# Gathering the token rows of a mixture of experts with three bf16 products in place of one fp32 product

## The reference

```python
lg = t @ wg                                  # 4 group logits
gi = argmax(lg); gp = softmax(lg)[gi]        # one group for each token
le = (t @ we).reshape(S, 4, 8)[gi]           # 8 expert logits of that group
tv, ti = top_k(softmax(le), 2)               # two experts for each token
cw = one_hot(gi * 8 + ti) * (tv / sum(tv) * gp)
gu = einsum('sd,edf->sef', t, w_gu)
hid = silu(gu[..., :256]) * gu[..., 256:] * cw
y = einsum('sef,efd->sd', hid, w_down)
```

## Time and profile before

| what | us |
|---|---|
| median of 3 runs | 1324.32 |
| lowest and highest | 1315.74, 1326.11 |
| profiled execution, time | 1324.0 |
| profiled execution, span on the core | 1321.8 |
| PE busy | 1131.9 (86%) |
| DVE busy | 542.0 (41%) |
| ACT busy | 341.3 (26%) |
| POOL busy | 56.4 (4%) |
| mean granted clock of PE | 0.938 of 2.4 GHz |

### The profile page before, as it was taken

How to read it: one execution, slowest core, us unless ns; L and a number is a source line. 1 busy time by engine, 2 the same in 40 slices (tenths; PEclk the granted TensorE clock), 3 DMA queues, 4 the chain that set the end, 5 groups by cost and what they waited for, 6 DMA issues and landing times.

```text
span 1321.8 us, 23637 instructions
## 1 busy us (share of the span) xinstructions
PE 1131.9 (86%) x9653; PEld 659.4 (50%) x9653; DVE 542.0 (41%) x1424; ACT 341.3 (26%) x650; POOL 56.4 (4%) x66
## 2 busy tenths in 40 slices
PE   5579998878887968689999999789795899999995
PEld 2146665556666935444444444567572534444433
DVE  3431194424341162624444444524337235444434
ACT  1112240121111211323233332234303233323322
POOL 2000000000000000000001000000000000000100
PEclk9789998999898979789999999899797999999997
DMA  8533115776775054009999996300622089999941
GB/s 249 171 127 121 71 64 177 277 258 238 259 261 205 4 221 191 1 10 425 421 425 425 423 417 249 135 12 1 255 103 89 0 349 423 428 426 420 422 199 40
DMA packets 45977, 297.21 MB, mean 225 GB/s; under 512 B 5956, under 2 KB 7336, under 8 KB 22344
## 3 DMA queue, kind: packets, MB, share of 16 engines
q1 hardware_dynamic: 43856, 290.17, 55.3%
q0 software_dynamic: 1840, 5.79, 1.9%
q10 hardware_dynamic: 200, 0.06, 0.0%
HBM read 293.77 MB, written 2.24 MB: 224 GB/s over the span
## 4 chain that ended last, share of the span: by engine, by line
PE 75%; DMA 11%; DVE 9%; ACT 2%; issue 2%; SPq 0%; ACTq 0%; DVEq 0%; POOL 0%; POOLq 0%
PE bank L686 73%; DMA ring<-in_ada_w 9%; DVE work L1501 2%; DMA ring<-in_kv_ada_w 2%; ACT work L1245 1%; DVE work L1507 1%; DVE work L1504 1%; DVE rstd L1539 1%; DVE x_res L1874 1%; DMA ring<-in_rw_w_rkv 1%; PE bank L1064 1%; DVE work L1860 1%; DVE ring L1501 1%; DVE work L1613 0%; PE bank L1231 0%
## 5 line engine op out<-in xcount | busy, mean ns | idle before, releaser
L686 PE MATMUL bank<-ring,work 128*64 128x512 f32 (+1 forms) x1760 | 351.3, 552 | 9.3 <-DVE work L1860 7.6
L686 PE MATMUL bank<-work,ring 128*128 128x320 f32 (+3 forms) x1600 | 302.0, 367 | 30.6 <-DVE work L1501 8.4
L686 PEld LDWEIGHTS bank<-work,ring 128*128 128x128 f32 (+2 forms) x1600 | 214.0, 173 | 118.5 <-issue 30.6
L686 PE MATMUL bank<-work 128*128 128x320 bf16 (+7 forms) x1906 | 227.0, 284 | 41.8 <-DVE work L1781 13.9
L686 PEld LDWEIGHTS bank<-ring,work 128*64 128x64 f32 (+1 forms) x1760 | 118.9, 138 | 218.3 <-issue 211.2
L686 PEld LDWEIGHTS bank<-work 128*128 128x128 bf16 (+3 forms) x1906 | 166.8, 126 | 113.2 <-issue 39.7
L1245 ACT ACTIVATE work<-bank 128x320 f32<-128x320 f32 (+6 forms) x111 | 55.8, 537 | 252.4 <-PE bank L686 235.8
L686 PE MATMUL bank<-ring 64*64 64x64 f32 (+2 forms) x2624 | 103.8, 233 | 2.1 <-issue 2.1
L686 PEld LDWEIGHTS bank<-ring 64*64 64x64 f32 (+2 forms) x2624 | 94.1, 144 | 21.8 <-issue 18.0
L686 PE MATMUL bank<-ring,cs 128*32 128x512 f32 x448 | 64.5, 661 | 39.9 <-DMA ring<-in_ada_w 33.9
L1874 DVE SCALAR_TENSOR_TENSOR x_res<-bank,mod,x_res 128x256 f32<-128x256 f32 (+1 forms) x256 | 86.1, 378 | 16.8 <-PE bank L686 2.7
(11 more groups left out here) (185 smaller groups left out, 754.3 us busy)
## 6 DMA issues: line engine op xcount, KB each, us to landing
ring<-in_moe_w_gu SPq DMA_DIRECT2D x64, 2048.0 KB, 13.5
ring<-in_moe_w_down SPq DMA_DIRECT2D x64, 1024.0 KB, 14.0
ring<-in_ada_w SPq DMA_DIRECT2D x40, 1024.0 KB, 5.3
ring<-in_rw_w_rkv SPq DMA_DIRECT2D x6, 2048.0 KB, 8.0
ring<-in_ada_w SPq DMA_DIRECT2D x4, 2048.0 KB, 28.6
ring<-in_kv_ada_w SPq DMA_DIRECT2D x8, 1024.0 KB, 4.9
ring<-in_rw_w_o SPq DMA_DIRECT2D x2, 2048.0 KB, 11.5
ring<-in_at_w_q SPq DMA_DIRECT2D x2, 2048.0 KB, 14.1
```

Source lines behind the costliest of these rows:

```text
L686: return eng.matmul(out, l, r, start=start, stop=stop, **kw)
```

## The change

`htok` is no longer an operand of a product. It is split into three bf16 parts, `hpart`, that add up to it: part 2 is `htok` rounded to bf16 (ACT), the remainder is written over `htok` (GpSimd), part 1 is the remainder rounded to bf16 (ACT), and part 0 is what is left after that (GpSimd). `pick` becomes bf16. PE multiplies each part by `pick` and adds up nine products in a bank where it added three, and it goes through the parts as its outer loop, so it opens all eight banks of a half before the first product. ACT makes part 2 of a token tile right behind the two copies of that tile, and takes the two exponentials behind tile 1 in place of behind tile 2.

```diff
@@ views
+        hpart = work[:, 0:9 * D // 2].bitcast(BF16).rearrange("p (s j d) -> p s j d", s=3, j=3)
-        pick = work[:, off[0]:off[0] + 3 * ROWS].rearrange("p (j s) -> p j s", j=3)
+        pick = work[:, off[0]:off[0] + 3 * ROWS // 2].bitcast(BF16).rearrange("p (j s) -> p j s", j=3)
@@ GpSimd, cleared(l)
                 pl.did(eng.memset(htok[64:128, 2, :], 0.0), ("htok padded", l))
+                pl.settle()
+                for j in range(3):
+                    pl.wait("hpart", l, 2, j)
+                    pl.did(eng.tensor_tensor(htok[:, j, :], htok[:, j, :], hpart[:, 2, j, :], ALU.subtract),
+                           ("hrest", l, j))
+                for j in range(3):
+                    pl.wait("hpart", l, 1, j)
+                    pl.did(eng.tensor_tensor(hpart[:, 0, j, :], htok[:, j, :], hpart[:, 1, j, :], ALU.subtract),
+                           ("hpart", l, 0, j))
@@ TensorE, moe(l)
                 for hf in range(2):
-                    for c in range(C):
-                        pb = bank.open("rows", l, c, hf)
-                        for j, (t0, kt) in enumerate(TILES):
-                            if c == 0:
-                                if hf == 0:
-                                    pe.wait("htok ready", l, j, 1)
-                                    if j == 2:
-                                        pe.wait("htok padded", l)
-                                pe.wait("picked", l, hf, j)
-                            ins = mm(pb[:, 0:T], htok[:, j, P * c:P * c + P], pick[:, j, T * hf:T * hf + T],
-                                     j == 0, j == 2)
-                        full(ins, "rows", l, c, hf)
+                    pbs = [bank.open("rows", l, c, hf) for c in range(C)]
+                    for part in (2, 1, 0):
+                        for c in range(C):
+                            for j in range(3):
+                                if c == 0:
+                                    pe.wait("hpart", l, part, j)
+                                    pe.wait("picked", l, hf, j)
+                                ins = mm(pbs[c][:, 0:T], hpart[:, part, j, P * c:P * c + P],
+                                         pick[:, j, T * hf:T * hf + T], part == 2 and j == 0, part == 0 and j == 2)
+                            if part == 0:
+                                full(ins, "rows", l, c, hf)
@@ ScalarE, moe(l)
                     for hf in range(2):
                         act(hrow[0:k, j, 64 * hf:64 * hf + 64, :],
                             pk("htok", l, j, hf)[0:k, :].rearrange("p (q c) -> p q c", c=C), ACT.Copy,
-                            ("read", "htok", l, j, hf), ("htok ready", l, j, hf))
-                ac.wait("group max", l)
-                ac.wait("top2", l)
-                act(rt[:, 6:9, 0:4], rt[:, 3:6, 0:4], ACT.Exp)
-                act(rt[:, 36, 0:3], rt[:, 35, 0:3], ACT.Exp, ("route exp", l))
+                            ("read", "htok", l, j, hf))
+                    if j == 2:
+                        ac.wait("htok padded", l)
+                    ac.settle()
+                    act(hpart[:, 2, j, :], htok[:, j, :], ACT.Copy, ("hpart", l, 2, j))
+                    if j == 1:
+                        ac.wait("group max", l)
+                        ac.wait("top2", l)
+                        act(rt[:, 6:9, 0:4], rt[:, 3:6, 0:4], ACT.Exp)
+                        act(rt[:, 36, 0:3], rt[:, 35, 0:3], ACT.Exp, ("route exp", l))
+                for j in range(3):
+                    ac.wait("hrest", l, j)
+                    act(hpart[:, 1, j, :], htok[:, j, :], ACT.Copy, ("hpart", l, 1, j))
```

## The result

The changed kernel has a median of 1344.08 us over 4 runs (1339.48 to 1349.14), the kernel before 1323.71 (1315.74 to 1326.11): a ratio of 1.0156, 95% interval 1.0111 to 1.0202. Run once more with the experiments it came out at 1344.01 us, ratio 1.0153 (1.0099 to 1.0208). The profiled execution took 1339.48 us, 15.5 us more than that of before.

The account below looks back on a forecast made before the run. PE's gathering, 28.13 us bare in each layer behind DVE's and ACT's chain, was taken to bound the stage. Start 3.5 (banks) + 11.4 us (turn-taking) later, work 22.0: 8.8 us a layer, 17.6 on 1324.0; forecast 1341, range 1317 to 1345.

Parts of the forecast that it names:

- What bounds the kernel: In the rows' gathering ACT, DVE and PE set the end in turn; 28.13 us of PE lie bare.
- The bf16 products: PE's gathering: 144 bf16 products take 19.5 us against 26.3 us for the fp32 ones, 6.8 us gained a layer.
- The slow start: PE's low clock at the start of gathering costs 1.8 us and stays.
- The banks: PE's first product waits for DVE's read of the ranks' bank, 3.5 us later; about 0.7 us between halves.
- ACT: Each new copy of 1024 columns takes 1.05 us; DVE's routing chain starts 0.5 us later.
- GpSimd: Six subtractions of 2.27 us each, 13.6 us, finish before PE needs them and are free if DVE is undisturbed.
- Turn-taking: GpSimd's subtractions stop DVE's two-SBUF-operand operations in the routing chain; in full, PE starts 11.4 us later; chance 0.52.
- The sum: PE's gathering ends at 587.0 against 578.2, 8.8 us later a layer; two layers give 17.6 us.
- Rival (a): GpSimd and DVE run side by side undisturbed: gathering ends 2.2 us earlier a layer, 1320 us; chance 0.32.
- Rival (b): GpSimd and DVE disturb each other in part: 1.4 to 5.4 us a layer, 1327 to 1335 us; chance 0.13.

Follow-up runs that it names:

- the bank read first: The changed kernel with DVE's last read of the ranks' bank put before the picks: 1328.09 us, ratio 1.0042; once more 1331.72 us, ratio 1.0051.
- short subtractions: The changed kernel with each of GpSimd's six subtractions cut to 2 of 1024 columns, gathered rows not exact: 1320.91 us, ratio 0.9982.

## Why the prediction was right

The forecast was 1341 us, slower, for one named reason; the time is 1344, and the reason holds. The time alone would not have shown that: the range, 1317 to 1345, takes in the case side by side as well, turn-taking in full was given no more than 0.52, and 1344 is near the range's upper end. It is the rows that tell the cases apart. By its steps:

- **What bounds the kernel.** Right: DVE's chain, ACT's exponentials and PE set the end of the stage in turn, and its length went to the span. ACT's copies are no longer on that path; DVE's operations before the exponentials are there in their place.
- **The bf16 products.** 0.138 us each in the second half (9.94 / 72) against 0.136. The slow start costs 12.33 - 9.94 = 2.4 us, not 1.8. PE takes 561.10 to 584.04, 22.9 us against the 22.0 worked out.
- **The banks.** Right in place and nearly in size: with the bank read first the stage is 3.1 and 3.3 us shorter, where 3.5 were put down less 0.4 for the reads. The pause between the halves is 0.68 us against 0.7.
- **ACT.** 1.06 us for a long copy against 1.05. With short subtractions the exponentials end 8.3 us into the stage, 0.5 later than before, as worked out.
- **GpSimd.** 2.12 us for a subtraction against 2.27. The first one started 0.14 us behind ACT's part: the 6 us that the Trainium skill ("GPSIMD Engine Reference", section 2.1) puts on a first call don't show; GpSimd had idled 15.11 us before it, in which they could be hidden. Part 0 is ready at 555.74, 5 us before PE starts.
- **Turn-taking.** The mechanism is right; the term is mis-sized. PE's start is 27.35 - 18.57 = 8.8 us late by it. The 11.4 us of the prediction hold ACT's 0.5 us too, so they stand against 9.3: the exponentials are 2.8 us late, not 3.3, and the four subtractions in a row cost DVE 6.5 us, not 8.1. The subtractions are shorter, and the last two of them cost DVE 1.4 us each instead of 2.0, because operations with a PSUM operand and reductions fill the time beside them. The argument for the upper end, that DVE has a second way into SBUF for a second operand or for speed, fits what the runs show: GpSimd's reads hold both kinds of operation, its fills only the fast ones with one operand.
- **The sum.** 8.8 us a layer were forecast, 7.7 and 7.6 measured in the stages: 15.3 instead of 17.6 us. Two errors partly cancel in it, 2.1 us too much turn-taking and 0.9 us too little for PE. What the forecast lacks is the 2.2 us outside the stages, 2.9 us of a slower clock in layer 1's loop less 0.7 gained elsewhere; with it the profiles account for 17.5 us, and the medians lie 20.4 apart. The second profile of the change has all of that, with a span of 1342.3 us: 15.4 us in the stages, 2.3 outside, and 2.9 ahead of them (538.5 against 535.6), which is scatter. So the time came out closer to the forecast than its terms deserve: what no term forecast happened to make up for the turn-taking that was put too high, and that is luck.
- **Rival (a),** side by side, is what the run with short subtractions shows: -0.7 and -1.8 us of stage where -2.2 was worked out.
- **Rival (b)** has a slip: a third of 11.4 is 3.8 us, which less 2.2 makes 1.6 us a layer, not 1.4. Nothing else hangs on it.

## What to carry to other kernels

Work that is handed to GpSimd because it is idle is not free while DVE runs a chain of small dependent operations: every one of them that reads two SBUF tiles, and every cast, can be held until a GpSimd instruction ends. Here six subtractions, 12.7 us in all, made PE start 8.8 us later. Look for who reads SBUF beside such a chain, or leave the arithmetic in PSUM, where PE can subtract a rounded part for 0.28 us a bank (six in 1.68 us). And when a loop opens several PSUM banks ahead of its first product, look at the last reader of each of them: here the wait for one bank took 3.1 to 3.3 us, half of the 5.9 us (28.12 - 12.33 - 9.94) by which the products got shorter.

## What the runs showed of the hardware

- A GpSimd instruction that reads SBUF (subtraction 2.12 us, copy 1.04 to 1.07 us) holds a DVE instruction with two SBUF operands, or a cast, until it ends (1.5 to 2.1 us for 0.16 to 0.26 in the change). Under fills of 1.8 us only one-operand DVE instructions waited: two casts (1.53 and 1.63 us for 0.21) and a `tensor_scalar` (0.34 for 0.16). With subtractions in a row, each held one such operation, which ended with it.
- An fp32 transposing product can be followed by one that adds to the same bank, if only the first transpose of the bank starts it anew. The Trainium skill, "PSUM — Partial Sum Buffer", section "The four PSUM rules", has the rule behind it: a start clears the marks of the whole bank, and what isn't marked is replaced. The two runs that differ in this flag agree: results wrong with it on all four transposes, right with it on the first alone.
- Behind the same 3.85 us with almost no work for PE, the same 32 products took 7.11 to 10.03 us, by the granted clock (1.00 in the fastest, 0.71 in the change), from kernel to kernel. In the two kernels that were profiled twice the time came out alike, 9.78 and 9.79 us, 7.11 and 7.11. What decides it is open.
